# Gate tiles of all chunks computed ahead of them, in blocks of seven products, and kept in DRAM

## The chip, the cores and the metric

One Trainium2 chip, one NeuronCore of it. The metric is the device time of one execution in microseconds (us). The kernel before took 2284.03 us (median of three runs, 2283.01 to 2284.37). Engine names: PE is TensorE, DVE is VectorE, ACT is ScalarE, POOL is GpSimd, SP is the engine whose queue issues nearly all DMAs. The kernel uses eight PSUM banks of 128 x 512 float32.

## The reference

One layer over 2048 rows of 1024 channels. Every row is normalised and multiplied by one wide input matrix; three mixers and three gates read the result.

```python
h = rmsnorm(x, norm_g)                       # 2048 x 1024
proj = h @ w_in                              # 1024 x (11*512 + 3*1024)
(a_val, a_gate, a_z, q, k, v, b_z, c_b, c_c, c_x, c_z, gates) = split(proj)
u = causal_depthwise_conv(a_val * sigmoid(a_gate), conv_a_w) + conv_a_b     # 31 taps
u = silu(layernorm(u, ln_a_g, ln_a_b));      y_a = (u * silu(a_z)) @ w_a_out
o = diff_attention(q, k, v, lam)             # causal, 4 heads, two softmaxes each
o = rmsnorm(o, subln_g) * (1 - lam_init);    y_b = (o * silu(b_z)) @ w_b_out
yc = c_b * causal_depthwise_conv(c_c * c_x, conv_c_w)      # 3 taps
y_c = (yc * silu(c_z)) @ w_c_out
g = sigmoid(gates + gate_b).reshape(s, 3, 1024)
x = x + (g[:,0]*y_a + g[:,1]*y_b + g[:,2]*y_c) @ w_o;      out = rmsnorm(x, final_g)
```

## The kernel before

Everything runs with channels on the partitions and rows on the free axis, in four chunks of 512 rows (`NCHUNK`, index c). Each float32 product is made of three passes in a rounded form: a tile is split into a rounded part (hi, an ACT copy) and the rest (lo, a subtraction on DVE or POOL), and PE multiplies hi by hi, hi by lo and lo by hi. A tile of 128 output channels over 1024 input channels is thus 8 x 3 = 24 matmuls of 512 columns (`row_part`), one over 512 input channels 12 (`y_part`).

Time inside a chunk is counted in steps (p, from 0 to `SPAN`); a step is four such matmuls, six steps (`PARTS`) are one weight tile. Each engine has a program of its own that walks through c and p and issues whatever falls on the step; the constants ending in `_LAG` and `_AT` say on which step each thing stands in its engine's queue, and semaphores do the rest. No queue reorders anything.

A chunk before has 88 weight tiles (`W_CHUNK`): 44 head tiles (four heads h of eleven: query, key, the a, b and c values and gates; 66 steps a head), then eight gate tiles of the a branch, then eight rounds of two gate tiles and one tile with y_b and y_c (`W_MID`), then four with y_a (`W_YA`), and eight of the output product (`W_FIN`, lines 811 to 832). The attention is laid between the matmuls of the head tiles: `scores` (L844, L860), `max_unit` and `exp_unit` (L1373, L1066), `scale_unit` and `combine` (L1077, L1419), `turn_a`, `turned_hi`, `turned_lo` (L869, L1086, L1426) and `times_v` (L893 to 896). More of it comes with every chunk, since chunk c attends to c + 1 blocks. The gate products share the two PSUM banks `PJ` with all other projections; ACT turns each into a tanh (`gate`, L1137), and DVE multiplies it with the y product (`product`, L1632, L1639).

The 31 taps of the a branch are 31 DVE instructions for each head and chunk (`conv_tap`, L1552, inputs and output in SBUF). `HEAD_TAPS` = (58, 46, 24, 0) of the 124 lie in the head stage of the chunks and the others in the gate stage behind it. They end before the layer norm over the four heads (`LN_AT`, step 408 or 414; `ln_means` L926, `ln_vars` L932, `ln_spread` L938, then `ln_apply`, `ln_product`, `za_hi_part`, and `za_lo_part` L1277 on POOL), which has to be done when y_a starts at step 456.

The weights come in chunk 0 from the input (`load_raw`), are split on ACT (L991) and on POOL (L1246, tiles 2 to 43) or DVE (L1342, the others), and the split form, 1 MB a tile, is stored in DRAM; later chunks load it back (`load_split`), one tile every six steps into three slots. The rows of the next chunk are loaded, normalised and split near the end of each chunk (`x_square`, `x_full` L1363, `x_hi` L1002, `x_lo` L1370). The two first tiles of chunk 0 are computed k by k while their rows still come (`opening_part`).

## Time and profile before

| what | us |
|---|---|
| median of the three runs | 2284.03 |
| span of the profiled execution | 2281.1 |
| PE busy | 2257.2 (99%) |
| DVE busy | 1426.0 (63%) |
| ACT busy | 756.0 (33%) |
| POOL busy | 232.8 (10%) |

The profiled execution is one of its own; its span runs from the first to the last instruction on the core, and its 2281.1 us are what the sums are made against. Busy PE is drawn with modelled ends, so 99% says that it hardly ever had nothing to do, and not at what rate it worked; the rate is read from the chain of work, where a run of matmuls stands with its count.

### The profile page before, as it was taken

The page shows a single profiled execution, that of the slowest core. Times are in us where ns is not written, and L with a number is a line of the kernel's source. Part 1 is how long each engine was busy: PE and PEld are TensorE (multiplying, and loading weights), DVE is VectorE, ACT ScalarE, POOL GpSimd, SP SyncE. Part 2 cuts the span into 40 slices and gives each one's busy share as a digit, 9 for nine tenths or more (in the row PEclk, how much of TensorE's full clock was granted, in tenths as well). Part 3 has the DMA queues.
Part 4 walks back from the last instruction along what each step waited for, and adds up shares of the span by engine and source line. Part 5 has one row for each costly group of instructions (what it writes and reads, how often), then busy time and mean ns, then how long its engine had stood idle before and what let it go on. Part 6 is the DMA issues. An engine that isn't in the chain of part 4 may idle for free.

```text
span 2281.1 us, 29046 instructions
## 1 busy us (share of the span) xinstructions
PE 2257.2 (99%) x10822; PEld 1832.9 (80%) x10822; DVE 1426.0 (63%) x2706; ACT 756.0 (33%) x1610; POOL 232.8 (10%) x186
## 2 busy tenths in 40 slices
PE   7999999999999999999999999999999999999998
PEld 6888888878888888888788788888877787788886
DVE  4767667764666665564557667665556657677752
ACT  4333332342333331032344344102135455441121
POOL 3544400100000000010000000001000000000010
PEclk9999999999999999999999999999999999999999
DMA  8877788798566665566755565556765555545555
GB/s 315 288 265 265 270 289 290 273 342 321 166 203 183 181 175 183 190 254 238 263 185 170 166 199 156 169 196 239 257 258 144 179 161 168 156 136 183 187 193 201
DMA packets 99339, 493.53 MB, mean 216 GB/s; under 512 B 15360, under 2 KB 18304, under 8 KB 54144
## 3 DMA queue, kind: packets, MB, share of 16 engines
q1 hardware_dynamic: 90464, 488.90, 63.8%
q10 hardware_dynamic: 8736, 2.78, 0.6%
q8 instruction: 87, 1.43, 0.3%
q14 instruction: 52, 0.43, 0.1%
HBM read 378.37 MB, written 113.27 MB: 216 GB/s over the span
## 4 chain that ended last, share of the span: by engine, by line
PE 96%; DVE 2%; DMA 1%; issue 1%; ACT 0%; SPq 0%; DVEq 0%; ACTq 0%
PE PJ L769 75%; PE SC L828 6%; PE SC L860 5%; PE TB L869 3%; PE OB L893 1%; PE OB L894 1%; PE OB L828 1%; PE PJ L828 1%; PE OB L896 1%; PE OB L895 1%; PE TB L904 0%; DMA Wraw<-w_stream 0%; DMA PX<-x_t 0%; PE TB L920 0%; PE SC L769 0%
## 5 line engine op out<-in xcount | busy, mean ns | idle before, releaser
L769 PE MATMUL PJ<-hT,Wp 128*128 128x512 f32 x6480 | 1571.4, 394 | 0.5 <-DVE PX L1632 0.5
L769 PEld LDWEIGHTS PJ<-hT,Wp 128*128 128x128 f32 x6480 | 1189.5, 188 | 254.0 <-issue 17.7
L1552 DVE SCALAR_TENSOR_TENSOR ACCS<-UA,col,ACCS 128x512 f32<-128x512 f32 x464 | 350.7, 798 | 0.4
L1066 ACT ACTIVATE PX<-SC,negm 128x512 f32<-128x512 f32 (+3 forms) x320 | 196.2, 623 | 145.5 <-DVE negm L1381 143.6
L1426 DVE TENSOR_TENSOR ZA<-TB,ZA 128x512 fp32r<-128x512 f32 (+1 forms) x144 | 95.1, 660 | 177.0 <-ACT ZA L1086 176.0
L1381 DVE TENSOR_REDUCE negm<-SC 128x2 f32<-128x1024 f32 (+3 forms) x160 | 169.0, 1061 | 40.3 <-PE SC L860 37.6
L1086 ACT ACTIVATE ZA<-TB 128x512 fp32r<-128x512 f32 (+1 forms) x144 | 82.6, 574 | 321.8 <-PE TB L869 321.8
L1137 ACT ACTIVATE TG<-PJ,col 128x512 f32<-128x512 f32 x64 | 44.1, 690 | 351.2 <-PE PJ L769 351.2
L1419 DVE SCALAR_TENSOR_TENSOR PX<-PX,sc 128x512 f32<-128x512 f32 (+3 forms) x160 | 108.0, 695 | 51.0 <-ACT PX L1077 50.8
L828 PE MATMUL SC<-Wp,KM 128*128 128x512 f32 x384 | 121.5, 389 | 0.0
L1077 ACT ACTIVATE PX<-PX,sc 128x512 f32<-128x512 f32 (+3 forms) x160 | 98.9, 655 | 64.9 <-DVE sc L1408 44.6
L1246 POOL TENSOR_TENSOR Wp<-Wraw,Wp 128x1024 fp32r<-128x1024 f32 x42 | 106.0, 2524 | 126.1 <-ACT Wp L991 126.1
L860 PE MATMUL SC<-KM,ZA 64*128 64x512 f32 (+3 forms) x960 | 118.5, 379 | 0.0
L991 ACT ACTIVATE Wp<-Wraw 128x1024 fp32r<-128x1024 f32 x88 | 92.9, 1055 | 62.8 <-DMA Wraw<-w_stream 37.4
L860 PEld LDWEIGHTS SC<-KM,ZA 64*128 64x128 f32 x960 | 80.3, 184 | 39.2 <-issue 28.7
L769 PE MATMUL PJ<-ZC,Wp 128*128 128x512 f32 x384 | 93.1, 390 | 0.0
L769 PE MATMUL PJ<-ZB,Wp 128*128 128x512 f32 x384 | 92.7, 390 | 0.0
L769 PE MATMUL PJ<-ZA,Wp 128*128 128x512 f32 x384 | 89.1, 391 | 1.1 <-DVE CT L1632 1.1
L769 PEld LDWEIGHTS PJ<-ZA,Wp 128*128 128x128 f32 x384 | 71.5, 188 | 17.0 <-DVE Wp L1342 1.9
L769 PEld LDWEIGHTS PJ<-ZB,Wp 128*128 128x128 f32 x384 | 72.1, 188 | 15.4 <-issue 0.5
L828 PEld LDWEIGHTS SC<-Wp,KM 128*128 128x128 f32 x384 | 72.1, 188 | 15.1
L769 PEld LDWEIGHTS PJ<-ZC,Wp 128*128 128x128 f32 x384 | 71.9, 188 | 14.9
(192 smaller groups left out, 2037.4 us busy)
## 6 DMA issues: line engine op xcount, KB each, us to landing
Wp<-split_weights SPq DMA_DIRECT2D x264, 1024.0 KB, 4.8
split_weights<-Wp SPq DMA_DIRECT2D x88, 1024.0 KB, 4.9
Wraw<-w_stream SPq DMA_DIRECT2D x88, 512.0 KB, 5.9
...
```

The costliest lines, as they stand in the source:

```text
L769: mm = pe.matmul(pj(c, r)[:, :], wt, rhs[:, 1 if q == 1 else 0, k, :], start=(n == 0), stop=(n == 3 * ktiles - 1))
L828: mm = pe.matmul(FIN_BANKS[half][t], (mTl if q == 1 else mTh)[:, k, t * P:(t + 1) * P], Wp[:, weight_slot(c, w), 1 if q == 2 else 0, kk * ...
L860: mm = pe.matmul(SC[k][:, m, 0:w], QM[rows, ql, t * P:(t + 1) * P], KM[rows, kl, j * CHUNK:j * CHUNK + w], start=(n == 0), stop=(n == 2))
L991: act.activation(Wp[:, k, 0, :], Wraw[:, w % 2, :], ACT.Copy).then_inc(w_hi, 1)
L1066: a = act.activation(probs(c, h, t, j, m)[:, 0:w], SC[k][:, m, 0:w], ACT.Exp, bias=negm[:, t % 2, j, m:m + 1], accum_out=lsum[:, t % 2, j, ...
L1077: act.activation(probs(c, h, t, j, 0)[:, 0:w], probs(c, h, t, j, 0)[:, 0:w], ACT.Copy, scale=sc[:, t % 2, j, 0:1]).then_inc(half_done, 1)
L1086: act.activation(AT[:, u % 2, 0, 0:w], TB[:, 0:w], ACT.Copy).then_inc(at_hi, 1)
L1246: pool.tensor_tensor(Wp[:, k, 1, :], Wraw[:, w % 2, :], Wp[:, k, 0, :].bitcast(F32), ALU.subtract).then_inc(w_lo, 1)
L1381: dve.tensor_reduce(negm[:, t % 2, j, :], SC[k][:, :, 0:w], AX.X, ALU.max, negate=True).then_inc(negm_ready, 1)
L1419: dve.scalar_tensor_tensor(out=probs(c, h, t, j, 0)[:, 0:w], in0=probs(c, h, t, j, 1)[:, 0:w], scalar=sc[:, t % 2, j, 1:2], in1=probs(c, h ...
L1426: dve.tensor_tensor(AT[:, u % 2, 1, 0:w], TB[:, 0:w], AT[:, u % 2, 0, 0:w].bitcast(F32), ALU.subtract).then_inc(tb_free, 1)
L1552: a = dve.scalar_tensor_tensor(out=acc, in0=src, scalar=col[:, n:n + 1], in1=acc, op0=ALU.mult, op1=ALU.add)
```

## The change

- A gate stage stands ahead of the chunks. It makes all 24 x 4 gate tiles. Two gate tiles (256 output channels) are a pair; there are 12 pairs, done once for chunks 0 and 1 and once for chunks 2 and 3 (`NP` = 24 turns). The product of a pair with the rows of two chunks is a product of 2 x 2 blocks: two output tiles by two halves of the 1024 channels, and those by two chunks. Pairs 0 and 12 make it directly, with eight block products of 12 matmuls. The other 22 make it of seven block products and sums of blocks.
- The sums of weight blocks are made on POOL for every pair (four instructions, `weight_sums`), with the splits of four blocks; three more blocks are split on DVE, and all are rounded on ACT. The sums of row blocks (`block_sum`) and their splits are made once for each two chunks on DVE. The seven products lie in seven PSUM banks; `copy_first` on ACT and seven additions on DVE (`products_sum`) put the four results together, ACT makes the tanh, and SP stores it in DRAM (`gd`, 96 tiles of 256 KB).
- The split rows of all four chunks are stored in DRAM (`hd`, 4 MB each) and loaded back ahead of their chunk (`load_h`), in place of the normalisation near the end of the chunk before.
- A chunk has 64 weight tiles: 44 head tiles, four each with y_c, y_b and y_a, eight of the output product. The head tiles are put in another order (`tile_order`), so that a head has 54 steps and eight tiles follow. The attention moves with them: its last turn in chunk 3 stands on step 259, before on step 301. The gates come back from DRAM from step 257 on (`load_gate`); those of two branches lie in the place of the rows, which are done by then.
- The layer norm starts at step 274 and has to be done by step 312.
- Taps: head 0 of every chunk and head 2 of chunks 1 to 3 are done on POOL: the product by ACT in chunks 0 and 1 (`conv_scale`) and by POOL in chunks 2 and 3, the addition by POOL (`conv_add`). The other heads stay on DVE and all lie ahead of step 275.
- In chunk 0 POOL splits all weight tiles (`DVE_SPLITS` = 64).
- Small things: the query tile is double, the rooms of the attention's output are other ones, and the lags of all steps are new.

```diff
 W_SLOTS = 3
-W_GA = H * HEAD_TILES
-W_MID = W_GA + M_OUT
-W_YA = W_MID + 3 * M_OUT
+FIRST_TILES = 9
+W_YC = H * HEAD_TILES
+W_YB = W_YC + M_OUT // 2
+W_YA = W_YB + M_OUT // 2
 W_FIN = W_YA + M_OUT // 2
...
-SCORE_AT = 17
-SCORE_SPAN = 55
+SCORE_AT = (17, 17, 17, 17)
+SCORE_SPAN = (49, 49, 49, 49)
...
-LN_AT = (408, 408, 408, 414)
+LN_AT = (274, 274, 274, 274)
...
+GATE_LOAD_AT = 257
+GATE_LOAD_STEP = 2
+H_LOAD_AT = (Y_AT[0] - 12, Y_AT[0] + 12)
...
-HEAD_TAPS = (58, 46, 24, 0)
-DVE_SPLITS = 44
+DVE_SPLITS = W_CHUNK
+POOL_HEADS = ((0,), (0, 2), (0, 2), (0, 2))
+DVE_HEADS = ((1, 2, 3), (1, 3), (1, 3), (1, 3))
+SCALED_BY_ACT = (True, True, False, False)
+POOL_FROM = 4
+POOL_STEPS = (150, 90, 90, 90)
+DVE_FROM = 5
...
 def tap_table(c):
...
+    ends = [tile_step(h, AV) for h in DVE_HEADS[c][1:]] + [LN_AT[c] - 4 - DVE_FROM]
+    for h, end in zip(DVE_HEADS[c], ends):
+        a, b = tile_step(h, AV) + DVE_FROM, end + DVE_FROM
+        for k in range(TAPS_A):
+            table.setdefault(a + k * (b - a) // TAPS_A, []).append((h, k))
...
+GP = 12
+NP = 2 * GP
+A11, A12, S4_, S1_, S2_, S3_, A22 = range(SLOTS)
+MOVING = ("x11", "x21", "x22", "t1", "t2", "t3", "t4")
...
+            def load_gate(c, g, m):
+                if g == 2:
+                    sp.wait_ge(t_done, turns_before(c + 1))
                 else:
+                    sp.wait_ge(group_done, G_CHUNK * c + W_YC)
...
+                sp.dma_start(gate_tile(m, g), gd[c, M_OUT * g + m, :, :]).then_inc(gate_in[g][m // 4], 16)
...
+            def seven_part(n, i):
...
+                for k in range(HALF):
+                    if direct_pair(before):
+                        pe.wait_ge(hb_lo[name], HALF * s + k + 1)
+                    for q in range(3):
+                        mm = pe.matmul(G_BANKS[i], Wg[:, i, 1 if q == 2 else 0, k * P:(k + 1) * P],
+                                       HB[:, BLOCK[name], 1 if q == 1 else 0, k, :],
+                                       start=(k == 0 and q == 0), stop=(k == HALF - 1 and q == 2))
+                mm.then_inc(g_prod, 1)
...
+            for n in range(NP):
...
+                if direct_pair(n):
+                    direct_part(n, 0)
+                    if n == 0:
+                        spread_scales(1)
+                    direct_part(n, 1)
+                else:
+                    for i in range(SLOTS):
+                        seven_part(n, i)
             for c in range(NCHUNK):
-                if c > 0:
-                    pe.wait_ge(h_lo, KT * (c + 1))
+                pe.wait_ge(h_in, 128 * (c + 1))
...
+            def conv_scale(c, h, k):
...
+                wait(act, tap_added, n - 1)
+                tap = COL_CW + k + TAPS_A * h
+                act.activation(tap_room(c, h, k), U4[:, h, k:k + CHUNK], ACT.Copy, scale=col[:, tap:tap + 1]).then_inc(tap_scaled, 1)
...
-            def gate(c, m, g):
-                r = gate_group(m, g)
...
+            def weight_sums(n):
...
+                pool.tensor_tensor(SS[:, 0, :], a21, a22, ALU.add).then_inc(gs_ready, 1)
+                pool.wait_ge(gs_ready, k + 1)
+                pool.tensor_tensor(SS[:, 1, :], SS[:, 0, :], a11, ALU.subtract).then_inc(gs_ready, 1)
+                pool.tensor_tensor(SS[:, 2, :], a11, a21, ALU.subtract).then_inc(gs_ready, 1)
+                pool.wait_ge(gs_ready, k + 2)
+                pool.tensor_tensor(SS[:, 3, :], a12, SS[:, 1, :], ALU.subtract).then_inc(gs_ready, 1)
...
+            def conv_add(c, h, k):
+                n = pool_adds(c, h) + k - 1
+                if not SCALED_BY_ACT[c]:
...
+                    pool.tensor_scalar(tap_room(c, h, k), U4[:, h, k:k + CHUNK], col[:, tap:tap + 1], None, ALU.mult
+                                       ).then_inc(tap_scaled, 1)
+                pool.wait_ge(tap_scaled, n + 1)
+                if k > 1:
+                    pool.wait_ge(tap_added, n)
+                pool.tensor_tensor(UC[:, h, :], UC[:, h, :], tap_room(c, h, k), ALU.add).then_inc(tap_added, 1)
...
+            def products_sum(n, i):
...
+                dst = (CG[:, 0, :], UU[:, 1, :], CG[:, 1, :], CG[:, 1, :], CG[:, 2, :], CG[:, 3, :], CG[:, 2, :])[i]
+                a = (UU[:, 0, :], UU[:, 0, :], UU[:, 1, :], CG[:, 1, :], UU[:, 1, :], CG[:, 2, :], CG[:, 2, :])[i]
+                b = (PJ[1][:, :], GB, GE, TB[:, :], GD, GE, PJ[0][:, :])[i]
+                dve.tensor_tensor(dst, a, b, ALU.add).then_inc(g_add, 1)
```

## Rows read from the trace of the kernel before

**Rows 1.** The page: span, busy time of the engines, chain by engine.
```profile
span 2281.1 us, 29046 instructions
...
PE 2257.2 (99%) x10822; PEld 1832.9 (80%) x10822; DVE 1426.0 (63%) x2706; ACT 756.0 (33%) x1610; POOL 232.8 (10%) x186
...
PE 96%; DVE 2%; DMA 1%; issue 1%; ACT 0%; SPq 0%; DVEq 0%; ACTq 0%
```

**Rows 2.** Waits of PE: who for whom, us in total, times, longest; its longest row.
```profile
PE TB L840 <- DVE SZB L1354: 8.9, 3, 8.0
```

**Rows 3.** Chain in order of time: start us, length us, what and how many.
```profile
330.91 89.78 PE PJ L769 x396
...
1081.48 15.41 PE PJ L769 x68
...
1659.97 15.41 PE PJ L769 x68
...
2228.09 21.76 PE SC L828 x96
```

**Rows 4.** Opening: one piece of the chain, then two DVE instructions of the timeline.
```profile
28.09 2.04 PE SC L769 x9
...
22.38 0.74 DVE L1363 SCALAR_TENSOR_TENSOR PX<-PX,col,TB 128x512 f32<-128x512 f32 x1
23.04 0.68 DVE L1370 TENSOR_TENSOR hT<-PX,hT 128x512 fp32r<-128x512 f32 x1
```

**Rows 5.** Groups by line: busy us, mean ns; idle before and its releaser.
```profile
L1246 POOL TENSOR_TENSOR Wp<-Wraw,Wp 128x1024 fp32r<-128x1024 f32 x42 | 106.0, 2524 | 126.1 <-ACT Wp L991 126.1
...
L1137 ACT ACTIVATE TG<-PJ,col 128x512 f32<-128x512 f32 x64 | 44.1, 690 | 351.2 <-PE PJ L769 351.2
...
L1579 DVE TENSOR_TENSOR UC<-UC,TB 128x512 f32<-128x512 f32 x16 | 10.1, 681 | 7.4 <-PE TB L926 7.4
...
L1370 DVE TENSOR_TENSOR hT<-SZA,hT 128x512 fp32r<-128x512 f32 x12 | 8.2, 686 | 0.9 <-ACT hT L1002 0.8
```

**Rows 6.** Stretches: length, busy us of PE, PEld, DVE, ACT, POOL, clock, DMA.
```profile
14.70:306.00 291.30, 290.50 (x1369) 236.75 (x1370) 192.24 (x323) 114.35 (x210) 125.45 (x60) 1.00 0.81 282
...
1081.50:1415.00 333.50, 333.50 (x1710) 266.56 (x1710) 210.23 (x454) 140.64 (x353) 18.48 (x20) 1.00 0.61 189
...
1660.00:2030.00 370.00, 370.00 (x1946) 293.90 (x1944) 232.24 (x490) 177.93 (x449) 18.65 (x20) 1.00 0.57 173
```

**Rows 7.** Timeline (start us, us) of chunk 0: DVE first, then POOL.
```profile
155.31 4.04 DVE L1552 SCALAR_TENSOR_TENSOR ACCS<-UA,col,ACCS 128x512 f32<-128x512 f32 x2
...
160.46 2.96 DVE L1552 SCALAR_TENSOR_TENSOR ACCS<-UA,col,ACCS 128x512 f32<-128x512 f32 x1
163.34 0.68 DVE L1480 TENSOR_TENSOR KM<-PJ,KM 128x512 fp32r<-128x512 f32 x1
...
154.89 2.76 POOL L1246 TENSOR_TENSOR Wp<-Wraw,Wp 128x1024 fp32r<-128x1024 f32 x1 [1.76 <-ACT Wp L991]
157.62 1.18 POOL L1268 TENSOR_TENSOR ZB<-PX,ZB 128x256 fp32r<-128x256 f32 x1
158.77 1.74 POOL L1272 TENSOR_TENSOR ZC<-CT,ZC 128x512 fp32r<-128x512 f32 x1
160.48 2.38 POOL L1246 TENSOR_TENSOR Wp<-Wraw,Wp 128x1024 fp32r<-128x1024 f32 x1
```

**Rows 8.** One line late in the kernel: ns min/median/max; then a one-input POOL group.
```profile
L1552 DVE SCALAR_TENSOR_TENSOR ACCS<-UA,col,ACCS x116: 736/744/1234, 2024.8 to 2160.8; 128x512 f32<-128x512 f32 x116
...
L1283 POOL MEMSET mask<- 128x256 f32 x1 | 0.3, 318 | 0.0
```

**Rows 9.** Layer norm of chunk 3, its first matmul and last POOL line.
```profile
L926 PE MATMUL TB<-Y,onesn x2: 590/590/591, 2164.9 to 2165.3; 128*128 128x512 f32 x2
...
L1277 POOL TENSOR_TENSOR ZA<-UC,ZA x4: 1291/1733/1742, 2190.1 to 2197.2; 128x512 fp32r<-128x512 f32 x4
```

**Rows 10.** DMA of the last 115 us of chunk 0: stretch, columns as in group 6.
```profile
421.00:536.00 115.00, 113.35 (x501) 92.02 (x500) 79.50 (x125) 45.40 (x65) 9.52 (x9) 1.00 0.89 327
```

1175 lines of the change are left out of this document (781 added, 394 removed).

## The prediction

> **What bounds the kernel now.** I read the page first. PE is busy for 2257.2 of 2281.1 us and is 96% of the chain that ended last [rows 1]. The list of PE's waits comes next: its longest row is 8.9 us, all of it in the opening [rows 2]. So PE is the bound from about 15 us to the end, and what is taken from PE is gained, as long as the others keep up. The chain gives PE's price: 396 matmuls of 512 columns in 89.78 us, 0.2267 us each where nothing lies between them [rows 3]. DVE is at 63% over the span, but the stretches matter: in the head stages it is busy for 232.24 of 370 us in chunk 3 and 210.23 of 333.5 us in chunk 2, again 63% [rows 6]. That is the cover on which the change draws. The trace was taken on one execution of 2281.1 us, 2.9 us under the median of the three timed runs; I make the sum against the span and add 2.9 at the end.
>
> **The matmuls taken away.** The gates cost 24 tiles x 24 matmuls x 4 chunks = 2304. After it, two pairs cost 96 each and 22 pairs 84 each: 2040. That is 264 fewer, at 0.2267 us [rows 3]: **-59.9 us**. Everything else on PE keeps its count (44 head tiles, 24 y tiles of 12 matmuls, the output product, the attention).
>
> **Does the gate stage hold that price?** A pair of seven products takes PE 84 x 0.2267 = 19.0 us. Beside it DVE has seven sums from PSUM (0.68 each, as L1579 [rows 5]) and three splits (0.69, as L1370 [rows 5]): 6.8 us. ACT has a copy and seven roundings (I take 0.63 each) and four tanhs of 0.69 [rows 5]: 7.8 us. POOL has four sums and four splits of 512 elements at 1.29 to 1.74, as L1277 [rows 9]: 10.3 to 13.9 us. DMA has 1 MB in and 1 MB out: 105 GB/s, against 327 GB/s in a stretch where PE hardly waits [rows 10]. All lie under 19.0, so PE stays the bound, at nothing added. Eight x tiles each for chunks 2 and 3 (0.74 each [rows 4]) fit beside pairs 6 to 9. The transition to pair 12 has no late link either: its row blocks are written while pair 11 runs, as each slot is given up. Without this cover a pair costs what its slowest engine needs; POOL's 13.9 would have to grow by 5 us before anything is lost.
>
> **The opening.** Now DVE paces it with 0.74 + 0.68 us a k tile [rows 4]. After it, two chunks have to be ready instead of one, before pair 1 can run at full speed. The second chunk's rows land at about 25 us (7 MB at 282 GB/s [rows 6]); its eight k tiles cost 11.4 us more on DVE while PE's 48 matmuls need 10.9, so PE ends pair 0 at about 43 us. Then t1 to t4 cost DVE 32 instructions of 0.69 = 22 us while pair 1 wants 19, with A12 behind t1 in DVE's queue (a wait of about 2.5 us) and t4 at the end (about 2.5 us). The loss grows from 19 us (48 matmuls of 10.9 us, done at 30.1 [rows 4]) to about 27: **+8 us**, between +4 and +15.
>
> **Chunk stages: where the cover goes.** The chunks lose a quarter of their matmuls, but only DVE's tap work and chunk 0's late splits shrink. All DVE taps must now end before step 270.
>
> *Chunk 3.* Before, no tap lies in its head stage. Now 62 do, at 0.744 us [rows 8]: +46 us, with about 10 us of attention that lay behind the stage and 3 us of first taps and sums. 232 + 59 = 291 us in a stage in which PE has 1056 matmuls (239 us) and the attention (chunk 3 from 1659.97 to 2228.09 + 43.5, less 2112 matmuls: about 133 us [rows 3]), 372 in all. That is 78%, but steps 0 to 24 and 240 to 264 carry little. Counted by the step tables with these durations, steps 72 to 240 hold about 228 us of DVE's own work against 245 us of PE: 93%.
>
> *The port.* In chunk 0 two taps that start at 155.31 take 4.04 us together, and one at 160.46 takes 2.96, ending 0.56 us behind the POOL instruction of 160.48 to 162.86 [rows 7]; the same tap takes 0.744 elsewhere [rows 8]. So a tap and a POOL instruction don't run together; one waits for the other's end, and some 0.15 to 0.2 us of the start of each is all that overlaps. DVE's reads of PSUM aren't held up. [...] In chunk 3 POOL does 60 additions (1.29 [rows 9]) and 60 products. No one-input product of this size is in the trace: by the memset of 256 elements in 0.318 us [rows 8] it is at least 0.6, by the two-input row at most 1.29; I take 0.65, nearer the one-input row. POOL is then active for about half of steps 28 to 118 and 136 to 226, and holds the port against DVE for about a third of them. About 170 DVE instructions of the port's kind fall there; a third of them meeting a hold of which 0.45 us is left makes 25 us. DVE's 228 become about 253 against 245: **+9 us** on PE in chunk 3, from 0 (PE's queue absorbs it) to +35 (products at 1.29, waits full). *Chunk 2* (1081.48 to 1659.97 [rows 3], so 100 us of attention): 195 own + 25 against 222: **+2** (0 to +15). *Chunk 1* (no products on POOL): 0 (0 to +5).
>
> *Chunk 0.* POOL splits at 2.4 us a tile and adds 30 taps over 150 steps; DVE has 93 taps at one in two steps. In steps 96 to 192 POOL holds about 67 us and DVE's instructions of the port's kind about 56, of 103 us of PE; less the overlapping starts, 102. The port is full. In chunk 0 before, POOL's 125 us of 291 [rows 6] and DVE's part came to about 80% in the worst blocks, and PE didn't wait [rows 2]. Behind POOL's late additions stand its splits of the next weight tile, with about 7 us in hand, and ACT's `conv_scale`, which waits for `tap_added` with exponentials and weight roundings behind it; PE waits for both. **+9 us** (0 to +28).
>
> **The layer norm.** In chunk 3 it takes from 2165.3 to about 2198.7 [rows 9], 33.4 us. In the new place it has 38 steps of 0.907 = 34.5 us, with sixteen products (0.69, or 1.4 with the sum) around it in DVE's queue instead of four; POOL's last splits meet DVE's products. PE's queue holds the three small products of the norm, so a late DVE stops everything behind them. **+2 us** a chunk: +8 (0 to +20).
>
> **DMA in chunk 0.** From step 257 to the end 18 tiles of 1.5 MB, 6.3 MB of gates, 4.2 MB of rows and some 6 MB more are 44 MB in 115 us, 383 GB/s; the rows show 327 GB/s at a share of 0.89 [rows 10], so 367 at 1. 120 us against 115, eased by the stalls above: **+3** (0 to +16). SP's new waits (`load_gate` for the last turn, step 259; the loads of weights are queued behind it) come one or two steps after it and cost nothing while the three slots are full; each step of lag there beyond about ten would stop PE.
>
> **Sum.** -59.9 + 8 + 9 + 2 + 9 + 8 + 3 = -20.9; 2281.1 - 20.9 = 2260.2; with 2.9, **2263 us**.
>
> **Rivals.** *A, DVE and the port are the new bound in the chunks (slower than before).* Place: steps 72 to 240 of chunks 2 and 3 and 96 to 192 of chunk 0. Price: +28 in chunk 0, +15, +35 and +5 in the others, +20 for the norms, with the opening +8: +111 - 60 = +51 at the end, 2335; it decides from a sum of stalls of 60 us on, at which the result is 2284. I take 2310 as its middle. For it: 93% own load, the doubled taps of rows 7. Against it: in chunk 0 before, DVE does `key_lo` only at 163.34, behind both long taps [rows 7], and PE waits for nothing. *B, the cover holds.* Only the opening costs: 2281.1 - 59.9 + 8 + 2.9 = 2232; with 3 for the norms 2235. For it: PE lost next to nothing beside stretches of 80% port load; the lags are new for each chunk. Against it: no row shows DVE above 69% [rows 10]. *C, the gate stage doesn't run at PE's pace* (the change doesn't do what it says): if a pair takes 21.8 us as a direct one does, the 60 us are gone and the opening and stalls stay, 2320. For it only POOL's 13.9 of 19.0.
>
> **How the numbers follow.** Chances: the forecast (2245 to 2279) 0.42, B (2228 to 2245) 0.22, A (2280 to 2335) 0.32, C 0.04. The range from 2232 to 2312 leaves out the lowest part of B and the upper part of A and C. A run of three can tell about 0.2% (4.6 us) from no change. Faster than 2279.5: B and nearly all of the forecast, 0.64; within 4.6 us 0.07; slower 0.29.
>
> **What would show it.** Right: matmuls of the gate stage at 0.227 us each and a stage that ends at about 490 us; PE's waits now named in the head stages on DVE's maxima, `turned_lo` and splits; L1552's successor with a mean over 0.9 us while its median stays at 0.745; POOL instructions of 1.3 us stretched. The chunks then take about 30 us more than their matmuls and attention. Wrong: waits of PE under 10 us in all (B), or over 60 (A); POOL's one-input product far from 0.65 us; a gap of PE between pairs (C); or the norm's wait at step 286 or 312 longer than 5 us in each chunk.

## The result and the profile after

The changed kernel takes **2372.8 us** (median of four runs, 2367.3 to 2378.3) beside 2283.8 us of the kernel before: a ratio of 1.039, 95% interval 1.0377 to 1.0402. It is slower, where 2263 us and faster were forecast. Its profiled execution spans 2376.5 us. Run again twice with no edit it took 2353.2 and 2354.7 us (below); the first figure is the highest of three, and all edits are compared with the second, which is called the control. Of all executions below one, of e4, took 7794.7 us, for which no row gives a cause; without it e4's median is 2310.0 us instead of 2310.8.

The page of the changed kernel: the span; busy time of each engine; the granted clock in 40 slices; the chain that ended last, by engine and by line.

```profile
span 2376.5 us, 30151 instructions
PE 2242.0 (94%) x10558; PEld 1803.6 (76%) x10558; DVE 1600.8 (67%) x2737; ACT 911.7 (38%) x1892; POOL 1020.1 (43%) x712
...
PEclk9899999999999999999999999999999999999999
...
PE 65%; DVE 18%; DMA 8%; issue 5%; POOL 2%; ACT 2%; SPq 0%; ACTq 0%; DVEq 0%; POOLq 0%
PE PJ L987 31%; PE SC L1051 10%; PE SC L1093 5%; PE PJ L1051 5%; DMA output_scales<-ost 5%; DVE ACCS L2010 3%; PE SC L1129 3%; PE TB L1051 2%; DMA Wraw<-output_scales 2%; PE TB L1138 2%; PE SC L1025 1%; DVE PX L1864 1%; DVE negm L1826 1%; PE OB L1162 1%; POOL Wp L1597 1%
```

PE was 96% of the chain [rows 1]; it is 65% now, and a fifth of the end is set by DVE. Two transfers stand in the chain by name that no step of the prediction mentions: the store and the load of the output scales. PE's waits, for the whole span (line and operation; us in total, times, longest):

```profile
PE OB L1162 <- DVE ZA L1871: 27.4, 12, 4.7
PE PJ L987 <- DVE CT L2089: 16.7, 10, 2.1
PE SC L1051 <- issue: 10.1, 1, 10.1
PE TB L1106 <- DVE XD L1757: 8.9, 3, 8.0
PE TB L1138 <- DVE VM L1932: 8.1, 5, 3.0
PE SC L1025 <- DVE HB L1776: 6.9, 4, 3.0
PE TB L1181 <- DVE ost L1899: 5.9, 1, 5.9
```

L1871 is `turned_lo`, L2089 the gate products of the y stage, L1932 `value_lo`. Before, the longest row of this list was 8.9 us, in the opening [rows 2].

The waits are not all that PE loses. Its granted clock:

```profile
core 0: 2376.5 us, clock 0.981
```

Before, it was 0.999. In the changed kernel's trace it falls from 1.0 to 0.5 of full speed twenty times, nineteen of them during a wait of PE or within 2 us of its end; the twentieth is at the very end. PE works for 71 us in these stretches; at half the clock that costs it up to 35 us, an estimate. All its waits together are 125 us, 14 before. So 111 us of waits and 35 us of clock are most of the 155 us of the table below; in the control they are 91 and 30 us of 130, in the last kernel of the list (e16) 40 and 9 of 54. The clock is a term that the prediction doesn't have.

**Where the time went.** The first and last matmuls of each kind bound the stages. Before, the four chunks last 521.2, 545.4, 578.5 and 611.6 us; less 576 matmuls of 0.2267 us (130.6 us) for each chunk they should last 390.6, 414.8, 447.9 and 481.0. By the same price the gate stage should last 2040 x 0.2267 + the 14.7 us of the start before = 477.2. With the tail that makes 2221.2 us, the span before less 59.9. Above these:

| us above the matmuls' price | gate stage | chunk 0 | 1 | 2 | 3 | sum |
|---|---|---|---|---|---|---|
| forecast | 8 | 14 | 2 | 4 | 11 | 39 |
| changed kernel | 32.3 | 43.6 | 35.7 | 17.9 | 25.8 | 155.3 |
| the same again | 30.2 | 41.0 | 25.6 | 12.4 | 20.4 | 129.6 |
| scales loaded late | 30.8 | 41.2 | 8.1 | 18.6 | 11.5 | 110.2 |
| all taps on DVE alone | 30.4 | 35.4 | 20.6 | 8.8 | 9.5 | 104.7 |
| all mends but the splits | 30.5 | 24.6 | 2.1 | 10.9 | 8.3 | 76.4 |
| and DVE splits all tiles | 30.3 | 6.7 | 2.9 | 12.4 | 8.3 | 60.6 |
| and the opening's order | 24.3 | 7.2 | 3.1 | 10.9 | 8.7 | 54.2 |

(The loss of the old opening behind its first 14.7 us, some 4 us, is in chunk 0 of before; and the gate stage holds sixteen small matmuls, another 4 us, which the chunks held before; so some 8 us of the gate stage's figure are not new, and the chunks' figures are too small by the same 8, chunk 0's by some 5 of them.) The forecast is spread with 2 us for each norm and 3 for the DMA. No single place is guilty: every stage is over its forecast. With those 8 us moved, the control is over it by 14 us in the gate stage, 32 in chunk 0, and 25, 10 and 9 in the others.

**The opening.** The timeline of the changed kernel from 48 us on (start, length of the group, engine, line, operation; in brackets the idle time before it and what ended it):

```profile
49.36 0.68 DVE L1800 TENSOR_TENSOR Wg<-SS,Wg 128x512 fp32r<-128x512 f32 x1
49.96 2.48 DVE L1794 TENSOR_TENSOR TT<-XF,TT 128x512 f32<-128x512 f32 x4
50.00 19.14 POOL L1618 TENSOR_TENSOR Wg<-SS,Wg 128x512 fp32r<-128x512 f32 x3 [5.93 <-ACT Wg L1275]
...
53.30 2.88 PE L1051 MATMUL TB<-HB,Wg 128*128 128x512 f32 x12
...
60.20 2.48 DVE L1794 TENSOR_TENSOR TT<-XF,TT 128x512 f32<-128x512 f32 x4
...
65.01 0.68 DVE L1816 TENSOR_TENSOR CG<-UU,PJ 128x512 f32<-128x512 f32 x1
65.61 1.16 DVE L1800 TENSOR_TENSOR Wg<-Wr,Wg 128x512 fp32r<-128x512 f32 x1
...
66.32 5.89 PE L1051 MATMUL SC<-HB,Wg 128*128 128x512 f32 x13 [10.14 <-issue]
```

The first of the three splits takes 16.22 us, to 66.22, and PE stands for 10.1 us for it. DVE has no pause in all this time. What is new at 65.01 is the kind of its instruction: the 25 that start from 49.96 on have two inputs in SBUF, this one has one there and one in the PSUM bank `PJ`, and GpSimd's split ends 1.21 us after its start, about the length of one split.

*The port* is the prediction's word, and stands here only for what the traces show: beside an instruction of GpSimd's with two inputs in SBUF, one of DVE's with two inputs in SBUF is held up, and the other way round (the split of 16.22 us). In the changed kernel's trace a tap takes 0.743 us on average where it meets nothing of GpSimd's (122 of them) and 1.21 us where it meets one or more of its additions and nothing else (24). DVE's sums from PSUM (L1816, one input there) are not held up: 0.673 to 0.690 us beside GpSimd's two-input instructions (100 of them), 0.675 to 0.689 without (54). Nor does GpSimd's power of 128x2 (L1645) hold a tap: 0.740 to 0.752 us in 20 meetings.

The long split in the line's own view (ns: smallest, median, largest):

```profile
L1618 POOL TENSOR_TENSOR Wg<-SS,Wg x66: 1272/1293/16218, 50.0 to 488.8; 128x512 fp32r<-128x512 f32 x66
```

The engines by stretch (its length; busy us and instructions of PE, PEld, DVE, ACT and POOL; granted clock, DMA share, GB/s):

```profile
50.00:75.00 25.00, 14.86 (x54) 11.72 (x53) 16.77 (x28) 11.15 (x20) 24.69 (x8) 0.73 0.43 140
100.00:300.00 200.00, 200.00 (x892) 165.91 (x891) 112.51 (x183) 95.02 (x159) 100.95 (x80) 1.00 0.47 160
```

In the first stretch PE issues 54 matmuls in 25 us; the granted clock over it is 0.73, since it is 0.50 from 58.8 to 72.4 us; the 13 matmuls from 66.32 us on take 5.89 us there, 0.453 us each. In the second, 892 matmuls in 200 us are 0.224 us each: the stage itself holds the price that was forecast.

**The round trip of the scales.** What stands in ACT's queue in chunk 1:

```profile
1025.99 0.40 ACTq L1410 DMA_DIRECT2D output_scales<-ost  x1
...
1035.19 0.34 ACTq L1416 DMA_DIRECT2D Wraw<-output_scales  x1
1035.57 0.72 ACT L1301 ACTIVATE UC<-UA,col 128x512 f32<-128x512 f32 x1 [7.17 <-DMA output_scales<-ost]
...
1036.30 0.58 ACT L1390 ACTIVATE ZA<-TB 128x512 fp32r<-128x512 f32 x1
...
1039.76 0.50 PE L1162 MATMUL OB<-ZA,VM 128*128 128x512 f32 x1 [1.87 <-DVE ZA L1871]
```

ACT stores the scales of a pair (L1410), and `load_scales` has ACT wait until the store has landed before it loads them back (L1416). For 7.17 us nothing else of ACT runs; behind it stands `turned_hi` (L1390), on it `turned_lo`, on that PE. The waits list names DVE for it, which was only the last link. Each store takes long, though it is 1 KB; the last line of the view of L1410:

```profile
DMA to landing us min/median/max: 8.8/9.7/12.2
```

The text ahead of the prediction says only that "the lags of all steps are new". These are the ones that matter:

```diff
-STORE_LAG = (0, 14, 14, 13)
-BACK_LAG = (0, 24, 24, 24)
-ZB_LAG = (0, 32, 32, 32)
...
+STORE_LAG = (0, 15, 12, 12)
+BACK_LAG = (0, 18, 20, 20)
+ZB_LAG = (2, 26, 25, 22)
```

Chunk 1 had ten steps between store and load and has three, about 3.8 us at 334 us for 264 steps. In chunks 2 and 3 there are eight, 10.6 and 11.8 us, against a landing of 9.7 in the median. From the load to DVE's use of what it brings (`BACK_LAG` to `ZB_LAG`) there were eight steps, and there are eight, five and two; DVE's waits for the load, 26.2 us in this trace, stand there.

### The profile page after: what moved, and what is told of

It is laid out like the page before. It is cut to its first block, busy times and chain, and to the rows that moved or that the text cites. A ratio compares the mean times of both kernels' runs of the same rounds, so it can differ in the third digit from the quotient of the medians.

```text
span 2376.5 us, 30151 instructions
## 1 busy us (share of the span) xinstructions
PE 2242.0 (94%) x10558; PEld 1803.6 (76%) x10558; DVE 1600.8 (67%) x2737; ACT 911.7 (38%) x1892; POOL 1020.1 (43%) x712
## 4 chain that ended last, share of the span: by engine, by line
PE 65%; DVE 18%; DMA 8%; issue 5%; POOL 2%; ACT 2%; SPq 0%; ACTq 0%; DVEq 0%; POOLq 0%
PE PJ L987 31%; PE SC L1051 10%; PE SC L1093 5%; PE PJ L1051 5%; DMA output_scales<-ost 5%; DVE ACCS L2010 3%; PE SC L1129 3%; PE TB L1051 2%; DMA Wraw<-output_scales 2%; PE TB L1138 2%; PE SC L1025 1%; DVE PX L1864 1%; DVE negm L1826 1%; PE OB L1162 1%; POOL Wp L1597 1%
## 5 line engine op out<-in xcount | busy, mean ns | idle before, releaser
L987 PE MATMUL PJ<-hT,Wp 128*128 128x512 f32 x4224 | 1056.5, 400 | 6.7 <-DVE ZA L1919 3.4
L987 PEld LDWEIGHTS PJ<-hT,Wp 128*128 128x128 f32 x4224 | 781.2, 191 | 172.0 <-issue 17.7
L1633 POOL TENSOR_TENSOR UC<-UC 128x512 f32<-128x512 f32 x165 | 224.9, 1363 | 138.8 <-ACT UC L1301 129.6
L1051 PE MATMUL SC<-HB,Wg 128*128 128x512 f32 x1056 | 250.1, 393 | 12.5 <-issue 10.1
L1051 PEld LDWEIGHTS SC<-HB,Wg 128*128 128x128 f32 x1056 | 200.0, 190 | 55.4 <-issue 12.8
L2010 DVE SCALAR_TENSOR_TENSOR ACCS<-UA,col,ACCS 128x512 f32<-128x512 f32 x261 | 241.3, 934 | 0.8
L1390 ACT ACTIVATE ZA<-TB 128x512 fp32r<-128x512 f32 (+1 forms) x144 | 82.4, 572 | 241.3 <-PE TB L1138 223.6
L1628 POOL TENSOR_SCALAR UC<-UA,col 128x512 f32<-128x512 f32 x90 | 152.8, 1698 | 49.3 <-DVE UC L1965 49.3
L1618 POOL TENSOR_TENSOR Wg<-SS,Wg 128x512 fp32r<-128x512 f32 x66 | 102.0, 1550 | 150.3 <-ACT Wg L1275 150.2
L1871 DVE TENSOR_TENSOR ZA<-TB,ZA 128x512 fp32r<-128x512 f32 (+1 forms) x144 | 94.4, 655 | 65.1 <-ACT ZA L1390 64.2
L1051 PE MATMUL PJ<-HB,Wg 128*128 128x512 f32 x528 | 128.5, 393 | 1.8 <-DVE HB L1776 1.8
L1051 PEld LDWEIGHTS PJ<-HB,Wg 128*128 128x128 f32 x528 | 100.2, 190 | 23.2 <-issue 2.2
## 6 DMA issues: line engine op xcount, KB each, us to landing
turned_rows<-HB SPq DMA_DIRECT2D x8, 2048.0 KB, 10.5
```

The source lines that it names most:

```text
L987: mm = pe.matmul(pj(c, r)[:, :], wt, rhs[:, 1 if q == 1 else 0, k, :], start=(n == 0), stop=(n == 3 * ktiles - 1))
L1051: mm = pe.matmul(G_BANKS[i], Wg[:, i, 1 if q == 2 else 0, k * P:(k + 1) * P], HB[:, BLOCK[name], 1 if q == 1 else 0, k, :], start=(k == 0 ...
L1618: pool.tensor_tensor(Wg[:, i, 1, :], weight_source(n, i), Wg[:, i, 0, :].bitcast(F32), ALU.subtract).then_inc(gw_lo_p, 1)
L1628: pool.tensor_scalar(tap_room(c, h, k), U4[:, h, k:k + CHUNK], col[:, tap:tap + 1], None, ALU.mult).then_inc(tap_scaled, 1)
L1633: pool.tensor_tensor(UC[:, h, :], UC[:, h, :], tap_room(c, h, k), ALU.add).then_inc(tap_added, 1)
L2010: a = dve.scalar_tensor_tensor(out=acc, in0=src, scalar=col[:, n:n + 1], in1=acc, op0=ALU.mult, op1=ALU.add)
```

## Experiments

Two repeats of the changed kernel and fifteen edited ones, each timed in four runs (e15 and e16 in ten) beside the kernel before, whose median kept to 2284.0 to 2284.2 us. The expectations of e1 to e4 reckon from 2372.8 us; their results are read against 2353.2. The changed kernel's own runs spread over 10 us in one loading, so a difference of a few us between two medians says little, and the stages of the traces say more. The gate stage, where it isn't edited, lasts 506.6 to 509.6 us in thirteen traces, so a stage is known to some 3 us there. e4 and e8 leave taps out and e10 writes something other than the low parts; the three only price what they change.

| kernel | us | ratio to before, 95% |
|---|---|---|
| c_again, c_third: no edit | 2353.2, 2354.7 | 1.029 to 1.0327, 1.0277 to 1.0318 |
| e1: scales loaded late | 2334.8 | 1.0208 to 1.0238 |
| e2: all products of GpSimd's taps on ACT | 2354.0 | 1.0291 to 1.0322 |
| e3: all splits of pairs 1 and 13 on DVE | 2353.9 | 1.0282 to 1.0327 |
| e4: GpSimd's taps left out | 2310.8 | 1.0096 to 1.0136 |
| e5: DVE splits from tile 44 on | 2348.4 | 1.0266 to 1.03 |
| e6: e1, e2 and e3 | 2339.5 | 1.0229 to 1.0259 |
| e7: pauses in DVE's opening | 2356.0 | 1.0304 to 1.0339 |
| e8: e1 and e4 | 2302.3 | 1.0061 to 1.0097 |
| e9: e1, e5, chunk 0's taps on DVE | 2317.5 | 1.0127 to 1.0159 |
| e10: low parts of t1 to t4 against PSUM | 2347.4 | 1.0261 to 1.0293 |
| e11: e9 and the norm's last step on ACT | 2311.0 | 1.0097 to 1.0133 |
| e14: all taps on DVE, alone | 2326.9 | 1.0163 to 1.0197 |
| e12: e11 and all taps on DVE | 2299.6 | 1.0055 to 1.0085 |
| e15: e12 and all splits of chunk 0 on DVE | 2283.0 | 0.9988 to 1.0007 |
| e16: e15 and another order in the opening | 2278.4 | 0.9964 to 0.9984 |

### The changed kernel again

No edit, twice.

> The changed kernel itself once more, with no edit, beside the next ones on the same chip. The profiles of the single edits of the opening and of chunks 2 and 3 both show 13 us less in the head stage of chunk 1, which neither edit touches, so part of their gain may not be theirs. If the first figure holds (2372.8 us), both gains of 19 us stand; if this run comes out near 2355 us, they are mostly the spread of the changed kernel from one loading to the next, and only what differs from this run counts. I expect 2355 to 2375 us, with chunk 1's head stage as the part that varies (321 to 334 us), since the landing time of the stores of the output scales is in its path.

> The changed kernel a third time, with no edit. The first figure was 2372.8 us, the second 2353.2 us, and three edits that leave chunk 1 alone had its head stage at 321 to 327 us, as the second. If the spread lies with the chip or the hour, this run falls anywhere from 2350 to 2375 us; I expect 2350 to 2358, the first figure being the rare one.

Measured: 2353.2 us (2350.2 to 2360.8), just under the range expected, and 2354.7 us (2344.7 to 2354.7), inside it. So 20 us of the first figure come and go with the loading or the chip, which these runs don't separate; its chunk 1 lasts 450.5 us, in the two others 440.4 and 440.7. ACT's waits for the stores sum to 61.6 us in the first trace and 47.0 in the second, DVE's for the loads to 26.2 and 11.6. That fits the round trip as the part that varies. But the stores land after 9.7 us in the median in the first two traces and 10.0 in the third, so they aren't later in the first; the loads are, with 6.8 us against 6.0 and 5.8. Why is not known. Without this control the first readings of e2 and e3, "19 us faster" each, would have stood as proofs of two causes; against it both are worth nothing.

### e1: the scales are loaded late

```diff
-BACK_LAG = (0, 18, 20, 20)
-ZB_LAG = (2, 26, 25, 22)
-ZBHI_LAG = (4, 26, 26, 26)
-ZBLO_LAG = (2, 28, 27, 27)
+BACK_LAG = (0, 26, 26, 26)
+ZB_LAG = (2, 34, 34, 34)
+ZBHI_LAG = (4, 35, 35, 35)
+ZBLO_LAG = (2, 36, 36, 36)
```

> The changed kernel with the loads of the output scales 6 to 8 steps later (BACK_LAG 26, ZB_LAG 34, ZBHI_LAG 35, ZBLO_LAG 36 in chunks 1 to 3), so that the store has 11 steps or more to land before ACT asks for it. Theory R (the round trip through DRAM blocks ACT's queue): ACT's waits ended by the store, 61.6 us in the changed kernel, go to under 5 us, DVE's waits for the load (43 us) too, and the time falls by 15 to 40 us, nearly all in the head stages of chunks 1 to 3. Theory P (the port between DVE and GpSimd is what costs): the same waits go, but the time falls by less than 5 us, since ACT has slack.

Measured: 2334.8 us, 18.4 less than the control. Of all waits for these transfers one is left (first fence), and PE's list for chunk 1's head stage, where L1162 had 19.8 us in the first trace, is down to the lines of the second:

```profile
DVE Wraw L1911 <- DMA Wraw<-output_scales: 0.8, 1, 0.8
```

```profile
PE TB L1138 <- DVE VM L1932: 2.1, 1, 2.1
PE PJ L987 <- DMA Wp<-split_weights: 0.6, 1, 0.6
PE OB L1162 <- DVE ZA L1871: 0.5, 1, 0.5
```

Chunk 1 falls from 440.4 to 422.9 us, chunk 3 by 8.9; chunk 2 grows by 6.2, and is as long in e6 and e9, which have the same lags; no run gives the reason. Theory R holds, within its range. (Of the 43 us of DVE's waits in the expectation the trace has 26.2.)

### GpSimd's taps: e4, e8, e2, e6, e14

e4 leaves out `conv_add` and `conv_scale`, e8 does so with e1's lags.

> The changed kernel without the taps that GpSimd does: taps 1 to 30 of seven heads are left out, ACT's products for them too (210 additions of 1.29 us, 120 products of 1.57 us, 90 products on ACT). It prices what the taps off DVE cost as a whole. Theory P: the time falls by 45 to 70 us, and DVE is stretched by under 90 us in all instead of 246. Theory R: the time falls by under 20 us, and the waits of ACT for the stores stay above 50 us.

> The changed kernel with the late loads of the output scales and without GpSimd's taps 1 to 30 (left out, seven heads). Against the changed kernel run again (2353.2 us) the late loads alone gave -18.4 and leaving the taps out alone -42.4. Theory S (the two are separate costs, each in PE's waits): about 2293 us, the sum. Theory Q (both delay the same queue, DVE's and ACT's attention work, and either one alone takes away most of it): 2300 to 2311 us. In both, what is left over 2221 us (before less the 264 matmuls) is the opening, the norm beside the y stage and chunk 0: more than 60 us, so the kernel isn't faster than before even without these taps.

Measured: 2310.8 us (-42.4 against the control, just under theory P's range), with DVE stretched by 119 us in all, where theory P had under 90: some 67 us are left in chunk 0's head stage, beside GpSimd's weight splits. Theory R has its waits (50.8 us of ACT's), but not its time. I count as stretch, over all DVE instructions that overlap one of GpSimd's, the duration over the median of the same shape without overlap; the changed kernel has 246 us, 84 of them in chunk 0's head stage, 28, 44 and 44 in the others. With both edits 2302.3 us: theory Q. The two costs overlap: 18.4 and 42.4 make 50.9, not 60.8. Chunks 1 and 3 show it: the late loads take 17.5 and 8.9 us off them in the changed kernel, and 10.5 and 0.3 where GpSimd's taps are gone.

e2 asks which half of a tap costs, the product of 1.57 us or the addition of 1.29 us; e6 adds e1 and e3.

```diff
-SCALED_BY_ACT = (True, True, False, False)
+SCALED_BY_ACT = (True, True, True, True)
```

> The changed kernel with the one-input products of the taps of chunks 2 and 3 on ACT, as in chunks 0 and 1 (SCALED_BY_ACT all True). 120 GpSimd products of 1.57 us (188 us) become ACT instructions of about 0.6 us (75 us). Theory P: DVE's instructions in chunks 2 and 3 are stretched by about half of the 88 us of now, and the time falls by 8 to 25 us, all in those two head stages. Theory R: ACT's queue, which the round trip blocks, gets longer; the time stays within 5 us or rises.

> The three edits together: late loads of the output scales, all one-input products on ACT, and DVE's splits for pairs 1 and 13. If the three causes are separate, their gains add up: against the changed kernel run again, 38 us less the part of its spread, plus 6 to 13 for the products, plus 3 for the opening: 2310 to 2325 us. If they overlap (ACT's queue takes up the products only where the round trip doesn't block it), more than the sum; if ACT becomes late by the 120 products, less: about 2335.

Measured: 2354.0 us, nothing against the control, and 2339.5 us, 4.6 more than e1 alone and beyond the worst case expected; in e6 chunk 3's head stage lasts 382 us, in e1 375. Theory P fails here: 188 us less on GpSimd bring nothing. By the same count DVE's stretch in the control is 44 us in chunk 2 and 42 in chunk 3; in e2 it is 28 and 40. The control's trace shows part of the reason. The groups of these lines, with mean ns of one:

```profile
L1633 POOL TENSOR_TENSOR UC<-UC 128x512 f32<-128x512 f32 x165 | 225.8, 1368 | 131.8 <-ACT UC L1301 122.6
L1628 POOL TENSOR_SCALAR UC<-UA,col 128x512 f32<-128x512 f32 x90 | 153.0, 1701 | 49.8 <-DVE UC L1965 49.8
```

and one by one, of DVE's 261 taps 120 overlap nothing of GpSimd's and take 0.744 us on average; 13 overlap only a product: 0.946, at most 1.18; 27 only an addition: 1.17, at most 1.83; 12 only a weight split: 1.54, at most 2.90. The product is the longest of the small ones and holds DVE the least. That ACT's longer queue takes up what is gained fits e6, which loses time without the round trip too, but no run isolates it.

e14 undoes the part of the change that moved taps:

```diff
-POOL_HEADS = ((0,), (0, 2), (0, 2), (0, 2))
-DVE_HEADS = ((1, 2, 3), (1, 3), (1, 3), (1, 3))
+POOL_HEADS = ((), (), (), ())
+DVE_HEADS = ((0, 1, 2, 3),) * 4
```

> The changed kernel with one part undone: all 124 taps of every chunk are on DVE, none on GpSimd. GpSimd loses 210 additions (1.29 us), 120 products (1.57 us), ACT 90 products; DVE gets 210 taps of 0.744 us, 30 of them in chunk 0 and 60 in each of the others. Theory P (GpSimd's additions cost DVE about as much in waits as the taps cost DVE itself): DVE's busy time in the head stages of chunks 1 to 3 changes by less than 20 us each, and the time falls by 5 to 25 us against 2353.2. Rival D (DVE's own load is the limit, for which the taps were moved away): DVE passes 90% in chunk 3, PE waits more, the time rises by 10 us or more.

Measured: 2326.9 us, 26.3 less than the control, just beyond theory P's range. The head stage of chunk 3, control first, then e14:

```profile
1840.00:2224.00 384.00, 371.47 (x1956) 293.77 (x1955) 317.82 (x566) 186.38 (x461) 201.42 (x142) 0.99 0.53 163
```

```profile
1826.00:2199.00 373.00, 368.76 (x1956) 291.11 (x1955) 318.05 (x628) 186.31 (x461) 20.75 (x22) 1.00 0.55 168
```

This is the clearest pair of lines in the study. DVE does 62 instructions more, 628 for 566, in the same busy time, 318.05 for 317.82 us, and GpSimd is busy for 21 us in place of 201. Moving two heads' taps away took no time off DVE: it gave back in waits what it saved in work. The stage is 11 us shorter (8.5 against the third loading). Chunk 2 repeats it: 277.0 us with 517 instructions, 278.9 with 579. Chunk 1, where ACT makes the products and GpSimd only adds, doesn't quite: DVE is busy for 226.0 us with GpSimd's help and 241.2 without, so a third of the 44.6 us was saved there; yet the stage is 5 us shorter without.

### Chunk 0: e5, e9, e15

```diff
-DVE_SPLITS = W_CHUNK
+DVE_SPLITS = 44
```

> The changed kernel with chunk 0's weight tiles from 44 on split by DVE, as in the kernel before (DVE_SPLITS = 44); 16 GpSimd instructions of 2.4 to 2.8 us in the y stage and the output product go away, DVE gets 16 of about 1.35 us. Theory P (products and norm queue behind GpSimd's splits: DVE instructions of 2.8 to 2.9 us beside them): the y stage of chunk 0 goes from 86 us to 74 to 80, and the time falls by 6 to 12 us. Rival (DVE is too full there with the norm and the products whoever splits): the y stage stays at 86 us or grows, the time stays within 3 us or rises.

> The changed kernel with the late loads, DVE's splits from weight tile 44 on, and all 124 taps of chunk 0 on DVE (none on GpSimd there). DVE gets 30 taps of 0.74 us more (22 us), GpSimd loses 30 additions of 1.29 us and ACT 30 products. Theory P (in chunk 0 the shared port is full, and an addition costs 1.7 times on GpSimd what it costs on DVE): the head stage of chunk 0 goes from 302 to 288 to 296 us, the time to 2316 to 2324. Rival D (DVE's own load is the limit in chunk 0): the head stage grows to over 305 us, the time to over 2333.

e5 measured 2348.4 us (-4.7), the y stage of chunk 0 at 80.5 us instead of 86.0: P's direction, with both figures just short of its ranges. The 5.5 us of the stage are clear (85.8 to 86.0 in the three unedited traces), the 4.7 of the median are within the spread. e9, with `POOL_HEADS[0] = ()`, measured 2317.5 us, 17.3 under e1, of which the late splits are some 5; chunk 0's head stage 293.6 us against 302.3. Theory P. e15 goes to the end of it, `DVE_SPLITS = W_SLOTS` on top of e12:

> The run with all mends (2299.6 us), and chunk 0's weight tiles from the fourth on are all split by DVE (DVE_SPLITS = 3): GpSimd loses 41 splits of 2.4 us (98 us), DVE gets 41 of 1.32 us (54 us) and should lose most of the 77 us by which it is stretched in the head stage of chunk 0. Theory P: the head stage goes from 293 us to 278 to 286, the time to 2286 to 2293. Rival D (DVE's own load and its order: PE waits for the splits behind the attention's work): the head stage stays at 293 us or grows.

Measured: 2283.0 us (ten runs), 16.6 less than e12. The same stretch of chunk 0, e12 first, then e15:

```profile
508.00:780.00 272.00, 254.75 (x1214) 204.25 (x1213) 235.45 (x332) 97.87 (x190) 117.27 (x58) 1.00 0.75 261
```

```profile
508.00:780.00 272.00, 269.38 (x1296) 219.91 (x1295) 226.04 (x396) 103.25 (x198) 22.20 (x19) 1.00 0.80 280
```

DVE does 64 instructions more and is busy for 9 us less; PE gets 82 matmuls more into the same 272 us. The head stage falls from 293.4 to 274.9 us, beyond theory P's best case. At the median pitch that each kind of matmul has in the kernel before it should last 268.1 us, so it loses 6.8; the kernel before lost 7.0 up to the end of its first gate tiles, but all except 2.6 of that in its opening. A split costs GpSimd 2.4 us and DVE 1.32.

### The opening: e3, e7, e10, e16

e3 gives DVE all seven splits of the pairs behind a direct one; GpSimd then only makes the sums.

```diff
-                    weight_lo(n + 1, A11)
-                    weight_lo(n + 1, S1_)
...
+                    if not direct_pair(n):
+                        weight_lo(n + 1, A11)
+                        weight_lo(n + 1, S1_)
...
```

> The changed kernel with all seven weight splits of pairs 1 and 13 on DVE (GpSimd does four of them now; one took 16.22 us beside DVE's unbroken row of sums and splits). Theory O (GpSimd is starved by DVE): the wait of 10.5 us at 56 us goes, the clock doesn't fall to 0.69 behind it, and the time falls by 10 to 16 us, all of it before 90 us. Rival (DVE's own work of 32 instructions is too long there): DVE gets 5.5 us more work in the place, PE waits as long for t2 to t4 as now for S1, and the time stays within 3 us.

Measured: 2353.9 us, nothing. The rival's number, but not its reason: the wait of 10 us is gone, and a sum of GpSimd's for pair 2 (L1609) now takes 11.2 us beside DVE's row, so that PE waits for pair 2's first split. It ends, like the split of 16.22 us, 1.25 us after DVE starts its first instruction with an input in PSUM. Lines of e3, GpSimd's sum and PE's wait:

```profile
L1609 POOL TENSOR_TENSOR SS<-Wr x22: 1273/1294/11222, 31.4 to 467.9; 128x512 f32<-128x512 f32 x22
```

```profile
PE SC L1051 <- POOL Wg L1618: 5.3, 1, 5.3
```

e7 adds a wait of DVE for its own end behind each of the 32 sums and splits, `dve.wait_ge(t_sum, ...)` and `dve.wait_ge(hb_lo[name], ...)`.

> The changed kernel with one thing more: in the opening (and at pair 12) DVE waits for the end of each of the 32 sums and splits of t1 to t4 before it starts the next. No work is moved. Theory O (GpSimd gets the port only in a pause between DVE's instructions): GpSimd's instruction of 16.2 us shrinks to under 3 us, PE's wait of 10.5 us becomes 2 to 6 us, DVE's 32 instructions take 3 to 15 us longer. Rival (GpSimd waits for something else, the data of ACT or a slot): the long instruction stays, and the stage gets longer by the pauses, 3 to 6 us.

Measured: 2356.0 us (+2.9); the longest split of GpSimd:

```profile
L1618 POOL TENSOR_TENSOR Wg<-SS,Wg x66: 1291/1297/1811, 51.0 to 487.9; 128x512 fp32r<-128x512 f32 x66
```

16.22 us have become 1.81. Now the two engines take turns, and DVE's four sums, 2.48 us in a row before, take 5.92. So DVE's unbroken row is what held GpSimd, as theory O says, though a pause isn't the only thing that lets it in: in the timelines above one DVE instruction with an input in PSUM does. The kernel gains nothing, since what GpSimd gets DVE loses.

e10 takes the low parts of t1 to t4 against a PSUM bank, so that the 16 splits of each visit have one input less in SBUF:

```diff
-                dve.tensor_tensor(HB[:, BLOCK[name], 1, k, :], block_source(name, k),
-                                  HB[:, BLOCK[name], 0, k, :].bitcast(F32), ALU.subtract).then_inc(hb_lo[name], 1)
+                low = OB[:, :] if name[0] == "t" else HB[:, BLOCK[name], 0, k, :].bitcast(F32)
+                dve.tensor_tensor(HB[:, BLOCK[name], 1, k, :], block_source(name, k), low,
+                                  ALU.subtract).then_inc(hb_lo[name], 1)
```

> The changed kernel, in which the low parts of t1 to t4 are taken against a PSUM bank in place of the rounded tile: the 32 DVE instructions stay, with the same shape and length, but have only one input in on-chip memory outside PSUM; what they write isn't the low part, so the gates come out wrong. Theory O (pair 1 is late because the port which DVE and GpSimd share is full in this place: 33 us of work for 19 us of PE): the loss of the gate stage goes from 41 to 30 to 35 us, GpSimd's instruction of 16.2 us becomes shorter. Rival (DVE's own row of 35 instructions, 22 us, is what PE waits for, whatever GpSimd does): the loss stays within 2 us of 41.

Measured: the gate stage 499.7 us against 507.4, the kernel 2347.4 us (-5.8), GpSimd's longest split 3.1 us: theory O. The same number of DVE instructions of the same length, only fewer inputs in SBUF, gives 7.7 us: at least a third of the opening's loss is the port, since the sums still have both inputs in SBUF. For the rest DVE's own row is the likely cause, which no run isolates.

e16 combines e3's edit with one more: GpSimd makes the first split of pairs 2 and 14 before its four sums.

> The run before it, and in the opening and at pair 12 DVE makes all seven splits of pairs 1 and 13, and GpSimd makes the first split of pairs 2 and 14 before it adds the four sums. Theory: each visit gets back the 4 to 5 us that PE waited for that split, the gate stage goes from 508 to 499 to 503 us. Rival (the shared port is full there, order only moves the wait): 506 to 509 us.

Measured: 2278.4 us (ten runs) against 2283.0; the gate stage 501.5 against 507.5 us. That is within the range expected, for both parts together; e3 alone had taken 1.3 us off the stage, no more than unedited traces differ.

### The norm: e11, and all together: e12

```diff
-                dve.tensor_scalar(UC[:, h, :], UC[:, h, :], col[:, COL_LG + h:COL_LG + h + 1],
-                                  col[:, COL_LB + h:COL_LB + h + 1], ALU.mult, ALU.add).then_inc(ln_n, 1)
...
+                act.activation(UC[:, h, :], UC[:, h, :], ACT.Identity, scale=col[:, COL_LG + h:COL_LG + h + 1],
+                               bias=col[:, COL_LB + h:COL_LB + h + 1]).then_inc(ln_n, 1)
```

> The kernel of the run with chunk 0's taps on DVE, and in it the last step of the layer norm's application (times gain plus bias, 4 instructions of 0.55 us a chunk) on ACT. Theory N (DVE is full in the y stage: about 35 us of products and norm in 34.5 us, so each us taken from it comes back): the second part of the y stages (5.8 us lost in chunks 1 to 3, 12 to 15 in chunk 0) loses 2 to 3 us less each, the time falls by 6 to 12 us against that run. Rival (the chain of the norm between the engines sets it, not DVE's load): ACT adds a step to the chain, the time stays the same or rises by up to 4 us.

> All mends together: late loads of the output scales, DVE's splits from tile 44 on, the norm's last step on ACT, and all taps on DVE in every chunk (the run with the norm's step on ACT, 2311.0 us, and 60 taps more on DVE in each of chunks 1 to 3). Theory P: 2298 to 2311 us, with chunk 3's stage the least sure of it. Rival D: 2320 us or more, lost in chunk 3 above all. Neither reaches the kernel before (2284 us), since the opening's loss of about 42 us and the y stages' stay.

e11: 2311.0 us, 6.5 less than e9; the y stages of chunks 1 to 3 fall by 1.6, 3.2 and 1.6 us, chunk 0's by 1.5. Theory N, with a smaller price: 2.2 us less of DVE's work bring about 1.6. e12: 2299.6 us, at the low end of theory P's range.

## Why the prediction was wrong, step by step

The sum has 39 us for all that PE loses; it lost 155 us, and 130 in the control. The matmuls were right. What failed, by size against the control: chunk 0's port (32 us over with its norm), the scales' round trip, which has no term (18), the opening (14), and the taps and norms of the other chunks. The clock, also without a term, adds to them all: up to 30 of the 130 us are lost because PE works for 60 us at a granted clock of 0.5 around its waits.

- **-59.9 for the matmuls, and the gate stage at PE's pace: right.** 892 matmuls in 200 us; from 75 to 300 us PE loses nothing. Rival C is out. The stage ends at 509.5 us and not at 490, by its opening.
- **The opening, +8 (bounds 4 to 15): mis-sized, 22 to 24.** Between 25 and 75 us PE loses 20 us of its pace, and some 4 to 6 more at pair 12, which was costed at nothing ("no late link"). The two waits of 2.5 us at A12 and t4 were sought in DVE's queue. The step that failed is that this part was summed engine by engine: DVE 22 us beside PE's 19. GpSimd's splits of pair 1 and sums of pair 2, eight instructions of 1.29 us, belong in the same sum, since the two don't run together (the split of 16.22 us): about 32 us. For the chunks the prediction says that a tap and a POOL instruction don't run together; it was not applied here.
- **The scales' round trip: missing.** It is the part that a reader could have had for nothing. The diff has the store 3 steps ahead of the load in chunk 1, where it was 10; the trace of before has its landing time, a median of 8.5 us; and the wait for it stands in ACT's own program, ahead of the attention's work (7.17 us of ACT's in the lines above). The prediction costed chunk 1 at 0, and it never names the DMAs that ACT issues. 18.4 us against the control, up to 38 against the first figure.
- **Taps on GpSimd relieve DVE: wrong.** The sum took DVE's tap work at 62 taps and added 25 us of waits for chunks 3 and 2, with 0 for chunk 1. No run shows these 25 us, or the 0.45 us a meeting that they were estimated from. Measured, DVE is stretched in the head stages by 84, 28, 44 and 44 us. For 60 taps moved (44.6 us of DVE's time) it gets about as much back in waits in chunks 2 and 3 (e14: 317.8 against 318.1 us). That the forecast of chunk 3 looks good is luck: its 291 us of own work and 25 of waits are 316, and 317.8 were measured, but as some 276 and 42 by the count of stretch above. Less 4.5 us for the norm, chunks 3, 2 and 1 are 16, 8 and 21 us over their price in the control, where +9, +2 and 0 stood; with the scales loaded late (e1) they are 7, 14 and 4.
- **The product of one input, 0.65 us between 0.6 and 1.29: wrong, and of no account.** It takes 1.57 us, above the upper bound, which had been the row of two inputs [rows 9]. The norm's one-input instruction of the same size takes DVE 0.55 us. But e2 and e6 show that moving it away brings nothing.
- **Chunk 0, +9 for the port, +3 for DMA: mis-sized, the largest error: +41 to +44 with its norm, and some 5 more by the note under the table.** The count of the port, 102 of 103 us, was right as a warning and was then priced at 9, since before had worked at 80% without a wait. e15 shows what it was: with splits and taps on DVE the head stage lasts 274.9 us instead of 302.1, of which the taps are 8.7 (e9) and the splits 18.5. Of the DMA no wait of PE names it for more than 0.8 us in any trace of the list.
- **The norm, +2 a chunk: the place right, the size too small.** The y stages of chunks 1 to 3 lose 5.6 to 5.9 us (before: 1.1 to 1.4), chunk 0's 18.7, of which e5 ascribes 5.5 to GpSimd's splits. PE's 16.7 us on the products (L2089) are this place.
- **SP's `load_gate`: right.** No wait of PE leads to it.
- **The rivals.** A (0.32) had the sign and the place, DVE and the port; its price of 111 us fell short of 130 to 155, since it had neither the round trip nor the clock, and the opening at 8. Its mark, PE's waits over 60 us, came out with 125 and 105; so did a mark of the forecast, L2010's mean of 0.934 us beside 0.744 undisturbed, which doesn't tell the two apart. B (3 us lost in the chunks) holds in no run: even e15 loses 30 there, which is the forecast's 31 by another way. C's 2320 leaves out the 2.9 us that A and B add.

**What is left open.** Why one loading of the same kernel is 20 us slower, and whether that lies with the chip. The 11 us of chunk 2 and 8 of chunk 3 that stay in e16; their head stages have waits at `value_lo` (5.2 us) and at the sums of squares (3.0). The opening's last 24 us.

e16 is the only one faster than the kernel before: 2278.4 us, 0.26% less (0.16 to 0.36). So the 60 us of matmuls were there; the change paid for them with an opening that no run filled, with a round trip given too few steps, and with work moved to an engine whose additions hold up the one to be relieved (a tap 1.21 us instead of 0.743).
